# Query splits and the output weights' low halves moved to GpSimd, output product in pieces: a hybrid decoder layer on one Trainium2 core

## The reference

```python
h = x @ w_in
o_a = rmsnorm(gated_delta_rule(q_a, k_a, v_a, g, beta)) * silu(z_a)     # 4 heads x 128, chunked recurrence
c = rmsnorm(ckv)
lat = dsa_attention(q_abs, c, q_i, k_i, w_i)    # per query the 256 keys that an indexer scores highest, ALiBi bias, softmax
o_s = (lat @ w_uv) * silu(z_s)                                          # 4 heads x 64
o_m = softmax(q_m @ k_m / 8) @ v_m * silu(z_m)                          # 4 heads x 64, 256 memory tokens
y = concatenate([o_a, o_s, o_m]) @ w_out
x = layernorm(alpha * x + y) * ln_g + ln_b
```

## Time and profile before

| | us |
|---|---|
| median of 3 runs (lowest, highest) | 867.44 (865.66, 868.85) |
| the profiled execution | 868.49 |
| its span | 866.7 |

### The profile page before, as it was taken

One profiled execution on the slowest core, in us unless ns is written; L12 is line 12 of the kernel. 1 busy time (PEld: TensorE's weight loads), 2 busy tenths in 40 slices (PEclk: granted clock), 3 DMA queues, 4 the chain that ended last, 5 costly groups with the idle time before them and its releaser, 6 DMA issues.

```text
span 866.7 us, 11346 instructions
## 1 busy us (share of the span) xinstructions
PE 759.9 (88%) x3940; PEld 625.8 (72%) x3940; DVE 505.9 (58%) x1084; ACT 464.9 (54%) x1030; POOL 144.8 (17%) x248
## 2 busy tenths in 40 slices
PE   6999969899987999699996999975887998897975
PEld 5888858688976889588895788853566766675763
DVE  5634958756674475634655377685556456536532
ACT  5533565889768875878777751335443333233300
POOL 0000000152021510232101520001002023203330
PEclk9999979999997999989996999998788998999998
DMA  9312110124010330015000251108402223112201
GB/s 355 100 49 73 48 37 26 36 65 140 25 50 26 97 107 25 25 54 150 25 26 25 77 164 49 55 13 305 137 13 74 71 63 103 49 56 85 85 24 49
DMA packets 63912, 65.86 MB, mean 76 GB/s; under 512 B 16368, under 2 KB 49392, under 8 KB 63472
## 3 DMA queue, kind: packets, MB, share of 16 engines
q1 hardware_dynamic: 63856, 65.13, 23.3%
HBM read 48.35 MB, written 16.78 MB: 75 GB/s over the span
## 4 chain that ended last, share of the span: by engine, by line
PE 55%; issue 17%; DVE 15%; ACT 12%; POOL 1%; DMA 0%; DVEq 0%; ACTq 0%; POOLq 0%
PE bank L926 17%; PE bank L934 8%; PE bank L936 8%; PE bank L935 8%; ACT cst L1756 3%; PE bank L940 3%; PE bank L1199 3%; DVE score L1364 2%; PE bank L1084 2%; PE bank L1097 1%; PE bank L1112 1%; PE bank L1110 1%; DVE qkvT L1475 1%; DVE qkvT L1476 1%; ACT arena L1673 1%
## 5 line engine op out<-in xcount | busy, mean ns | idle before, releaser
L934 PE MATMUL bank<-x_hi,ring_split 128*128 128x512 f32 x480 | 200.3, 417 | 8.3 <-DVE x_lo L1309 7.4
L936 PE MATMUL bank<-x_hi,ring_split 128*128 128x512 f32 x480 | 191.7, 399 | 0.0
L935 PE MATMUL bank<-x_lo,ring_split 128*128 128x512 f32 x480 | 191.3, 398 | 0.0
L1756 ACT ACTIVATE cst<-score,sel 128x1024 bf16<-128x1024 f32 (+2 forms) x192 | 166.8, 873 | 28.9 <-DVE sel L1386 27.4
L934 PEld LDWEIGHTS bank<-x_hi,ring_split 128*128 128x128 f32 x480 | 93.3, 194 | 24.7 <-DVE ring_split L1317 7.4
L936 PEld LDWEIGHTS bank<-x_hi,ring_split 128*128 128x128 f32 x480 | 92.4, 193 | 20.4
L935 PEld LDWEIGHTS bank<-x_lo,ring_split 128*128 128x128 f32 x480 | 93.0, 194 | 15.6
L1869 ACT ACTIVATE arena<-arena,misc 128x512 f32<-128x512 f32 (+7 forms) x32 | 24.8, 775 | 71.2 <-DVE misc L1593 71.2
L926 PE MATMUL bank<-w_out_hi,mix_hi 128*128 128x512 f32 x128 | 56.2, 439 | 7.0 <-DVE mix_lo L1623 4.2
L1673 ACT ACTIVATE arena<-bank 128x512 f32<-128x512 f32 x77 | 44.1, 589 | 32.1 <-PE bank L940 13.5
L1643 DVE SCALAR_TENSOR_TENSOR arena<-qkvT,bank 128x512 f32<-128x512 f32 x16 | 11.0, 687 | 78.5 <-PE bank L926 78.5
(11 more groups left out here) (273 smaller groups left out, 1471.4 us busy)
## 6 DMA issues: line engine op xcount, KB each, us to landing
ring<-in_w_groups SPq DMA_DIRECT2D x30, 512.0 KB, 3.6
...
```

The costliest lines, as they stand in the source:

```text
L934: nc.tensor.matmul(dst, hi, xh, start=(c == 0), stop=False)
L935: nc.tensor.matmul(dst, hi, xl, start=False, stop=False)
L936: last = nc.tensor.matmul(dst, lo, xh, start=False, stop=(c == KT - 1))
L1756: sc.activation(signs[order[e] % 2][:, 0:w], score[:, score_at(b):score_at(b + 1)], ACT.Sign, scale=-1.0, bias=candidate[:, b - 2:b - 1], ...
```

## The change

Five edits, which come together:

1. `qsplit` goes to POOL: a copy to hi and a subtraction. There are two hi buffers now (even and odd turns), and the step is placed almost a turn earlier: the queries that turn n+1 scores are split at the end of turn n-1, those of blocks 3 and 4 together before the loop. The odd buffer lies over `stage`.
2. The subtractions of `split out*` go to POOL. ACT still makes the hi halves.
3. `y` is cut into four pieces of six matmuls. The pieces of the first half lie between the attention units, each with a list entry of its own; of the second half three come before `o` and one behind it. DVE takes up a half after its fourth piece.
4. The scores of a head stay one unit, and without `qsplit` as their first unit they move a little forward.
5. In the loop, banks are dealt anew: `pT`, `mixT`, `mpT`, `msc` share banks 4 to 6 ("A"), `lat` and `o` have bank 0 ("O"), `y` has 1 and 7 ("Y"), the scores alone have 2 and 3.

```diff
@@ make_plan
-                    steps += [... [("kh", 1, 1), ("qsplit", first_block)]][b]
+                    steps += [... [("kh", 1, 1), ("qsplit", first_block), ("qsplit", BLOCK_ORDER[1])]][b]
...
     def output(b):
-        return [[("mixT", b, 0), ("mixT", b, 1)], [("mix_split", b)], [], [("y", b, 0)]]
+        return [[("mixT", b, 0), ("mixT", b, 1)], [("mix_split", b)], [], *[[("y", b, 0, s)] for s in range(4)]]
+
+    def second_half(b):
+        return [("y", b, 1, s) for s in range(4)]
...
-            queues.append((0.5, [[("qsplit", nb)], scores(nb, 0), *[scores(nb, h) for h in range(1, SAH)]]))
+            queues.append((0.5, [scores(nb, h) for h in range(SAH)]))
...
-        if n:
-            add(("y", BLOCK_ORDER[n - 1], 1))
-        add(("o", b))
-    for e in [*normalise(BLOCK_ORDER[-2]), *sum(output(BLOCK_ORDER[-1]), []), ("y", BLOCK_ORDER[-1], 1), *normalise(BLOCK_ORDER[-1])]:
+        if n + 2 < NB:
+            add(("qsplit", BLOCK_ORDER[n + 2]))
+        last = second_half(BLOCK_ORDER[n - 1]) if n else []
+        for e in [*last[:3], ("o", b), *last[3:]]:
+            add(e)
+    for e in [*normalise(BLOCK_ORDER[-2]), *sum(output(BLOCK_ORDER[-1]), []), *second_half(BLOCK_ORDER[-1]), *normalise(BLOCK_ORDER[-1])]:
@@ banks
-           "msc": "D", "mixT": "D", "y": "L", "pT": "D", "lat": "P", "mpT": "D", "o": "P"}
+           "msc": "A", "mixT": "A", "pT": "A", "mpT": "A", "lat": "O", "o": "O"}
-        pools = {"P": (0, 1), "L": (2, 3), "D": (4, 5, 6, 7)}
+        pools = {"P": (0, 1), "L": (2, 3), "D": (4, 5, 6, 7), "A": (4, 5, 6), "O": (0,), "Y": (1, 7)}
@@ tensor engine, y
+                    for c in (2 * s, 2 * s + 1):
+                        mh, ml = mix_hi[:, c * P:(c + 1) * P], mix_lo[:, c * P:(c + 1) * P]
+                        nc.tensor.matmul(ps(key)[:, :], mh, wout_hi[:, c, half], start=(c == 0), stop=False)
+                        nc.tensor.matmul(ps(key)[:, :], mh, wout_lo[:, c, half], start=False, stop=False)
+                        last = nc.tensor.matmul(ps(key)[:, :], ml, wout_hi[:, c, half], start=False, stop=(c == KT - 1))
@@ gpsimd (the two steps are gone from vector and, for qsplit, from scalar)
+                elif k == "qsplit":
+                    n = PLACE[e[1]]
+                    pool.wait_ge(*queries_loaded(n))
+                    if n == 0:
+                        pool.wait_ge(*filled(("M", DNH - 1, 1, NLEV - 1)))
+                    elif n == 1:
+                        pool.wait_ge(side_stored, 16 * len(staged))
+                    else:
+                        before = BLOCK_ORDER[n - 2]
+                        pool.wait_ge(*filled(("sc", before, SAH - 1, len(idx_chunks(before)) - 1)))
+                    link(g.tensor_copy(q_hi(n), q_raw(n)))
+                    g.tensor_tensor(q_lo(n), q_raw(n), q_hi(n).bitcast(F32), ALU.subtract).then_inc(head_queries_split, 1)
+                elif k == "split" and e[1][:3] == "out":
+                    name = e[1]
+                    pool.wait_ge(weights_hi_ready, order[e])
+                    g.tensor_tensor(out_piece(wout_lo, name), out_piece(wout, name), out_piece(wout_hi, name).bitcast(F32),
+                                    ALU.subtract).then_inc(weights_split, 1)
```

More of the change, by code:

```diff
@@ L601, in build @@
         released_sem = [sem(f"released{i}") for i in range(8)]
-        bank_of, use_of, count = {}, {}, {k: 0 for k in pools}
+        bank_of, use_of, count, uses = {}, {}, {k: 0 for k in pools}, [0] * 8
         for e in plan:
@@ L606, in build @@
                 bank_of[key] = pools[pool][n % len(pools[pool])]
-                use_of[key] = n // len(pools[pool]) + 1
+                uses[bank_of[key]] += 1
+                use_of[key] = uses[bank_of[key]]
                 count[pool] += 1
@@ L1236, in _ @@
                 elif k == "y":
-                    b, i = e[1:]
+                    b, i, s = e[1:]
+                    key = e[:3]
                     if PLACE[b] == 0:
-                        pe.wait_ge(weights_split, order["split", f"out{4 * i + 3}"])
-                    if i == 0:
-                        pe.wait_ge(mix_split, PLACE[b] + 1)
-                    if not first(e):
-                        pe.wait_ge(*vacated(e))
+                        pe.wait_ge(weights_split, order["split", f"out{4 * i + s}"])
+                    if s == 0:
+                        if i == 0:
+                            pe.wait_ge(mix_split, PLACE[b] + 1)
+                        if not first(key):
+                            pe.wait_ge(*vacated(key))
                     half = slice(i * 512, (i + 1) * 512)
-                    pairs = []
-                    for c in range(KT):
+                    for c in (2 * s, 2 * s + 1):
                         mh, ml = mix_hi[:, c * P:(c + 1) * P], mix_lo[:, c * P:(c + 1) * P]
-                        pairs += [(mh, wout_hi[:, c, half]), (mh, wout_lo[:, c, half]), (ml, wout_hi[:, c, half])]
-                    group(ps(e)[:, :], pairs).then_inc(fill_of(e), 1)
+                        nc.tensor.matmul(ps(key)[:, :], mh, wout_hi[:, c, half], start=(c == 0), stop=False)
+                        nc.tensor.matmul(ps(key)[:, :], mh, wout_lo[:, c, half], start=False, stop=False)
+                        last = nc.tensor.matmul(ps(key)[:, :], ml, wout_hi[:, c, half], start=False, stop=(c == KT - 1))
+                    if s == 3:
+                        last.then_inc(fill_of(key), 1)
         @block.vector
@@ L1633, in _ @@
                         v.tensor_tensor(quad(mixT[1]), quad(ps(e)[:, :]), gate, ALU.mult).then_inc(release_of(e), 1)
-                elif k == "y":
-                    b, i = e[1:]
+                elif k == "y" and e[3] == 3:
+                    b, i = e[1:3]
+                    e = e[:3]
                     if i == 0:
```

37 lines of the change are left out of this document (13 added, 24 removed).

## The result

The changed kernel takes 871.6 us (median, 870.68 to 873.24), the kernel before 868.2 us beside it. The ratio is 1.0037, 95% interval 1.0024 to 1.0051: slower by 3 us, which is measurable but within 0.5%. Its profiled execution took 871.55 us with a span of 869.7 us.

A forecast was written before the change was run, and what follows sets the result against it. TensorE was taken to set the pace, so only its waits count. Terms -12 + 11 + 2.6 - 0.7 = +0.9 us against 867.44 gave 868.3 us; the forecast's own range was 864 to 872, with 860 to 877 overall.

The forecast's parts named there:

- part B: Starts of turns 2 to 7: the late layer-norm chain and `mix_lo` make TensorE wait; +11 us, ends +5 and +17.
- part A: Turns 0 and 1: subtractions leaving DVE end its mutual blocking with ACT; -12 us, ends -15 and -5.
- part D: The rest, chiefly one DVE instruction leaving the scan's chain before the loop: -0.7 us, upper end +2.
- rival 2: Turns 0 and 1 and turn starts: GpSimd's instructions hold DVE up; +10, 877 us; chance 0.28 together with rival 3.
- E: The time at which TensorE has finished both `y` and `o` of a turn.
- The 1.5 us that turn 7 was to lose behind `mix_lo`: Turn 7: 1.5 us more wait because the copy of key block 3 stands behind `mix_lo`.
- So the wait that was to go is replaced by one of nearly the same length: Starts of turns 2 to 7: the layer-norm wait, 2.8 us, replaces the query-split wait, 3.1 us.
- The clock: Turns 2 to 7: three more waits dropping the granted clock would take part B to its upper end, +17 us.
- Part C: The tail: the last block's DVE transposes stand behind L1651, starting 2.6 us later; +2.6 us, upper end +5.
- Rival 1: Turns 2 to 7 keep their length, layer norm's lateness hidden; about 860.5 us; chance 0.34 with its neighbours.
- Rival 3: Turn starts: the queries' splits come no earlier and TensorE still waits for them; 874 us; chance 0.04.
- The page on offloading: Whole kernel: shared-port warning; DVE losing all POOL subtraction time would make +8.9 of the -12 in turns 0 and 1.

The follow-up runs named there:

- run 4: The kernel before with only the eight low halves of the output weights moved to GpSimd: 863.73 us, ratio 0.9937.
- run 3: The changed kernel with the eight low halves of the output weights back on VectorE: 875.03 us, ratio 1.0069.
- run 10: The kernel of run 1 with the output weights' low halves back on VectorE: 852.41 us, ratio 0.9811.
- run 6: The kernel of run 1 with the queries' split back on ScalarE and VectorE, at the head of the next scores: 864.90 us, ratio 0.9955.
- run 8: The changed kernel with layer norm's gain and bias on GpSimd cut to 8 columns: 868.57 us, ratio 0.9994.
- run 1: Also called y_first: the changed kernel with all four pieces of the second output half in front of `o`, as before: 850.13 us, ratio 0.9782.
- run 9: The kernel of run 1 with the first output half in one piece of 24 products instead of four: 843.59 us, ratio 0.9706.
- run 11: The kernel before with only `o` put in front of the second output half: 893.05 us, ratio 1.0275.
- run 7: The changed kernel with products that nobody reads laid before three long waits, to raise the clock: 871.94 us, ratio 1.0033.
- Run 5: The kernel of run 1 with block 2's queries split after the second weight split of turn 0, not the fourth: 846.10 us, ratio 0.9742.

## Why the prediction was right, and where its reasons were not

The sum held within its range (868.3 forecast from 867.44, that is +0.9; +3.4 measured), and so did the sums of its parts. What failed is the composition of part B, and the cause given for part A.

- **Part A, -12:** `o` of turn 0 starts at 615.90 (forecast 617), the scores of turn 1 at 623.02 behind POOL (624.2), and turn 1 ends 12.0 us earlier, of which 0.75 is part D. The cause was put too simply. The splits alone give 5.3 us (run 4) and are worth 3.4 and 2.3 at the end (runs 3 and 10). The move of the queries' split gives nothing here (run 6: turn 1 ends 1.5 us earlier without it). The kernel with neither move and the other edits was not run, so where the rest of the 12 us comes from stays open. One candidate is a part of the edit that I had not named: in run 4 `y` waits 4.16 us for all four splits, and in the changed kernel each piece waits for its own. GpSimd does hold VectorE in turn 0 by rival 2's mechanism (a merge took 2.06 us, and two instructions over two columns, L1604, 0.90 and 1.68 us), only for few instructions.
- **Part B, +11:** turns 2 to 7 grew by 13.0. Turn 7 has 32.6 us (forecast 31), the others 29.6 to 32.1 (30 to 32), L1658 starts at E + 3.67 (3.7), and in turn 7 the transpose waits for its bank until 805.04 + 5.35 = 810.39, which is the forecast E + 5.35. L1598 takes 1.24, 1.12 and 0.98 us in turns 2, 4 and 6, and `mix_lo` 2.15 to 2.67 in turns 3, 5 and 7. By turn the fit is looser than in the sum: growths of 2.5, 0.9, 1.1, 0, 1.7 and 5.1 us were forecast and 1.6, 1.4, -0.4, 1.8, 2.1 and 6.5 measured. The 1.5 us that turn 7 was to lose behind `mix_lo` are not there: without GpSimd's hold it takes as long (32.65 us, run 8). The failed step is "So the wait that was to go is replaced by one of nearly the same length". It weighed both edits as one wait for another, but they are large terms: the queries' split a block ahead gives back 14.8 us (run 6), and `o` in front of the last piece costs 21.5 (run 1). The pieces, with the place that the merging rule gives them, cost another 6.5 (run 9). Turns 2 to 7 take 174.5 us before, 185.6 with the pieces, the banks and the weights' splits (run 6), 168.5 with the queries' split added (y_first) and 187.5 with `o` before the last piece: +11.0, -17.1 and +19.0. Taken in another order the shares differ (the order of `o` alone adds 20.7 to the kernel before, run 11). The prediction priced none of these three by itself, so that its +11 came near their sum of +13.0 is in part luck. I had seen that the first piece comes earlier and waits for `mix_lo`, but had not priced it apart.
- **The clock:** I gave it no us and the upper end 6. Run 7 puts its cost at 0.7 us in turn 2 and 1.8 in turn 6. Below full clock inside the waits it costs nothing.
- **Part C, +2.6:** the tail from E on takes 21.7 us against 19.6, +2.1.
- **Part D, -0.7:** POOL's scaling in turn 0 starts at 610.79 instead of 611.54, -0.75.
- **Rival 1** (the turns keep their length) fell: they grow, and it takes `o` behind `y` to undo that (run 1). **Rival 2** fell as a whole: its mechanism is there, but all of layer norm's hold costs 3.0 us (run 8), and part A kept its 12. **Rival 3** fell: no wait for the queries' split in turns 2 to 6.
- **The page on offloading.** The Trainium skill (Perfetto Trace Analysis, Optimizing Scalar/DVE Operations) warns that moving work between VectorE and GpSimd may not help. Here it helped: the weights' splits on GpSimd shortened, by the medians, all three kernels in which they were tried (runs 3, 4 and 10), and so did the queries' split, moved and placed a block ahead (run 6). In the trace GpSimd's work met few of VectorE's instructions with both operands in SBUF; that this is why it helped is argued, not shown. Where it met one, that took up to 2.3 us, so the warning's reason is seen in runs 4 and 8.

The sum of the runs in order: 868.6 before; 843.6 with both moves to GpSimd, new banks, the first half whole, the second in pieces and `o` last (run 9); 850.1 with the first half in pieces (run 1); 871.6 with `o` before the last piece. The fastest kernel measured is run 9, 2.9% under before. Run 5's edit on top of it was not tried, nor was it sought why the turns 3 to 5 of run 6 are longer than before's.
